# Products of weight and one-hot for every other chunk moved from VectorE to GpSimd, in the first of two gate builds

## What is computed

```python
def peer_ffn(xn, w_query, sub_keys, expert_u, expert_v):   # 16384 experts
    ...   # 8 heads; top 16 of 128 x 128 keys: expert_idx and gates, 128 per token
    u = expert_u[ib]                                  # rows gathered by token
    act = jax.nn.gelu(jnp.einsum('ced,cd->ce', u, xb))
    return jnp.einsum('ce,ced->cd', gb * act, expert_v[ib])
```

## Time and profile of the kernel before

| | us |
|---|---|
| three runs | 2079.51, 2079.55, 2066.76 |
| their median | 2079.51 |
| the profiled execution | 2073.71 |
| span in its profile | 2072.0 |

### The profile page before, as it was taken

The page is one execution under the profiler, slowest core; times in us unless marked ns, Lnnn a source line. Parts: engine busy times, 40 slices in busy tenths (PEclk is TensorE's granted clock), DMA queues, the critical chain, the costliest instruction groups (busy, mean ns, idle before and its releaser), DMA issues.

```text
span 2072.0 us, 23875 instructions
## 1 busy us (share of the span) xinstructions
PE 1931.7 (93%) x8967; PEld 1250.0 (60%) x8967; DVE 1206.6 (58%) x3046; ACT 414.7 (20%) x963; POOL 876.8 (42%) x785
## 2 busy tenths in 40 slices
PE   8999999999989999998898498999999889999998
PEld 7688886855865888884767376444435543333333
DVE  0123101002997888887886999978768784444321
ACT  2233210121202454121211122100003330101102
POOL 0000000000775433543445555654657777556643
PEclk9999999999989999999999558999999999999999
DMA  7343444433999887999897768999999999999997
GB/s 250 105 134 110 143 162 134 130 122 122 344 391 355 299 265 240 376 386 328 326 315 287 279 214 264 337 409 409 409 409 353 369 355 400 409 409 409 409 389 284
DMA packets 252439, 613.47 MB, mean 296 GB/s; under 512 B 18676, under 2 KB 121124, under 8 KB 252324
## 3 DMA queue, kind: packets, MB, share of 16 engines
q0 software_dynamic: 110592, 402.70, 51.7%
q1 hardware_dynamic: 141120, 208.17, 28.7%
q10 hardware_dynamic: 612, 1.07, 0.2%
HBM read 609.77 MB, written 2.10 MB: 295 GB/s over the span
## 4 chain that ended last, share of the span: by engine, by line
PE 63%; DMA 16%; DVE 12%; POOL 4%; issue 2%; ACT 2%; SPq 0%; POOLq 0%; DVEq 0%; ACTq 0%
PE ps L595 27%; PE ps L853 10%; PE ps L816 8%; PE ps L608 7%; DMA u_rows<-in_peer_u_dram,idx 6%; DVE u_rows L1328 5%; DMA v_rows<-in_peer_v_dram,idx_turned 3%; POOL u_rows L554 2%; DMA wring<-in_w_in_dram 2%; PE ps L631 2%; DMA wring<-in_peer_w_query_dram 2%; PE ps L843 2%; POOL v_rows L568 2%; DVE hot_a L1382 2%; PE ps L620 1%
## 5 line engine op out<-in xcount | busy, mean ns | idle before, releaser
L554 POOL DMA_INDIRECT u_rows<-in_peer_u_dram,idx x512 | 596.4, 1165 | 1008.8 <-DVE idx L1315 520.6
L1328 DVE CUSTOM_DVE_ANT_0 u_rows<-u_rows,xn 128x1024 f32<-128x1024 f32 x512 | 622.0, 1215 | 173.1 <-DMA u_rows<-in_peer_u_dram,idx 169.7
L595 PE MATMUL ps<-xT,wring 128*128 128x256 f32 x2432 | 556.9, 388 | 23.4 <-DMA wring<-in_w_in_dram 11.0
L595 PEld LDWEIGHTS ps<-xT,wring 128*128 128x128 f32 x2432 | 465.6, 194 | 93.8 <-DMA wring<-in_w_in_dram 12.8
L853 PE MATMUL ps<-d_rows,gates 128*128 128x512 f32 x1024 | 456.0, 599 | 0.0
L853 PEld LDWEIGHTS ps<-d_rows,gates 128*128 128x128 f32 x1024 | 190.0, 190 | 266.0 <-issue 266.0
L816 PE MATMUL ps<-v_rows,diag 64*64 64x512 f32 x1928 | 248.8, 633 | 19.9 <-DMA v_rows<-in_peer_v_dram,idx_turned 15.5
L843 PEld LDWEIGHTS ps<-hot_b,hot_a 128*128 128x128 f32 x1024 | 148.4, 232 | 61.2 <-DVE hot_b L1390 31.3
L568 POOL DMA_INDIRECT v_rows<-in_peer_v_dram,idx x121 | 133.0, 1099 | 122.5 <-PE ps L816 100.8
L843 PE MATMUL ps<-hot_b,hot_a 128*128 128x64 f32 x1024 | 156.7, 320 | 24.6 <-DVE hot_b L1390 24.5
L816 PEld LDWEIGHTS ps<-v_rows,diag 64*64 64x64 f32 x1928 | 68.9, 138 | 157.2 <-issue 132.7
(11 more groups left out here) (197 smaller groups left out, 1711.5 us busy)
## 6 DMA issues: line engine op xcount, KB each, us to landing
wring<-in_w_in_dram SPq DMA_DIRECT2D x128, 512.0 KB, 5.6
d_rows<-in_peer_v_dram SPq DMA_DIRECT2D x128, 512.0 KB, 6.8
wring<-in_peer_w_query_dram SPq DMA_DIRECT2D x32, 512.0 KB, 8.2
wring<-in_w_branch_conv_dram SPq DMA_DIRECT2D x16, 512.0 KB, 6.4
wring<-in_w_branch_attn_dram SPq DMA_DIRECT2D x16, 512.0 KB, 5.9
wring<-in_w_out_dram SPq DMA_DIRECT2D x16, 512.0 KB, 6.4
wring<-in_xattn_wq_dram SPq DMA_DIRECT2D x16, 512.0 KB, 8.1
wring<-in_xattn_wo_dram SPq DMA_DIRECT2D x16, 512.0 KB, 6.5
```

What stands on the lines that cost most here:

```text
L554: pool.indirect_dma_start(out=u_rows[:, n % URING, :], out_offset=None, in_=peer_u[0], in_offset=bass.IndirectOffsetOnAxis(ap=experts_of(g ...
L595: mm = pe.matmul(bank(job)[:, 0:HN], w[:, k % 4, P * b:P * (b + 1)], act[:, k, :], start=(k == 0), stop=(k == KT - 1))
L1328: dve.tensor_tensor_reduce(out=u, in0=u, in1=(xn2 if h else xn1)[:, i, :], scale=1.0, scalar=0.0, op0=ALU.mult, op1=ALU.add, accum_out=dot ...
```

## The change

GpSimd makes the product of `hot_b` and the weights for the odd chunks 1, 3, ... 31 of the first build. It does so in its loop at n = CH_SLOT[ch] + 8, behind the u gather and the v gathers of that step; the gather of that step waits for the dot of slot CH_SLOT[ch], the slot in which VectorE makes the one-hots of ch. The product waits for `hot_half`. A new semaphore `hot_pool` counts GpSimd's products, and TensorE waits for one or the other. VectorE's one_hots ends for these chunks with the second one-hot. The second build is unchanged.

```diff
     CH_SLOT = spread(12, 46, 32) + spread(151, 177, 32)
+    BY_POOL = range(1, 32, 2)
...
+        def wait_hots(eng, ch):
+            if ch in BY_POOL:
+                eng.wait_ge(hot_pool, BY_POOL.index(ch) + 1)
+            else:
+                eng.wait_ge(hot_rdy, sum(c not in BY_POOL for c in range(ch + 1)))
+
+        def weigh(eng, ch):
+            i, o = 8 * (ch % 32) // P, 8 * (ch % 32) % P
+            eng.wait_ge(hot_half, ch + 1)
+            return eng.tensor_tensor(hot_b[:, ch % 2, :, :], hot_b[:, ch % 2, :, :],
+                                     wT[:, i, o:o + 8].unsqueeze(2).to_broadcast([P, 8, 64]), ALU.mult)
...
                     ).then_inc((v_ready if kind == "v" else u_ready)[place], 16)
+                for ch in BY_POOL:
+                    if CH_SLOT[ch] + URING == n:
+                        weigh(pool, ch).then_inc(hot_pool, 1)
...
             def gate_chunk(ch):
-                pe.wait_ge(hot_rdy, ch + 1)
+                wait_hots(pe, ch)
...
-                dve.wait_ge(hot_half, ch + 1)
-                dve.tensor_tensor(hot_b[:, ch % 2, :, :], hot_b[:, ch % 2, :, :],
-                                  wT[:, i, o:o + 8].unsqueeze(2).to_broadcast([P, 8, 64]),
-                                  ALU.mult).then_inc(hot_rdy, 1)
+                if ch not in BY_POOL:
+                    weigh(dve, ch).then_inc(hot_rdy, 1)
```

More of the change, by code:

```diff
@@ L379, in build_trunk @@
         hot_rdy = sem("hot_rdy")
+        hot_pool = sem("hot_pool")
         wb_done = sem("wb_done")
```

## The result

The changed kernel takes 2079.41 us (median of 22 runs); the kernel before, run beside it, 2072.77 (22 runs). The ratio is 1.0032 with a 95% interval of 1.0020 to 1.0044, that is +6.6 us (4 to 9): a small loss, clear of the noise. The median of the three runs that I started from (2079.51) lay high in the spread of before (2065 to 2088).

The account below looks back on a forecast made before the run. VectorE was taken to bound the first gate build, transfers what follows. Saving 11.5 us and losing 14.6 gave +3.1, so 2076.8 us from the profiled 2073.71, moved towards the three-run median to 2078; range 2061 to 2091.

Parts of the forecast that it names:

- VectorE sets the pace, transfers behind follow one to one: First build: VectorE busy 132.16 of 135 us; time saved or lost there moves everything behind by as much.
- Saved: 16 x 0.72 = 11.5 us: First build: 16 of 32 products leave VectorE, 0.72 us each, the most the change can bring.
- Exclusion is real, and most of its price is VectorE's: GpSimd's products and VectorE's two-input instructions make each other stand; VectorE loses 16 x 1.25 - 5.4 = 14.6 us.
- the walk: VectorE's 16 slots behind odd chunks, checked for one-input work that can run beside GpSimd's product: 5.4 us of cover.
- TensorE costed at nothing: First build: moved chunks ready about 1.7 us later, 0.9 us of slack at half clock, so no wait.
- Sum: Loss of 14.6 us less 11.5 saved gives +3.1, so 2076.8 us from the profiled 2073.71.
- the likeliest case: Exclusion with a small net cost, its own range 2071 to 2087 us; chance 0.50.
- rival B: Late products make TensorE the bound at half clock: +11, 2085 us, VectorE's waits 8 us or more; chance 0.12.
- B's upper form: TensorE's gaps also keep the clock low, 10 pairs' periods of 11.0 us for 8.8: another 22, 2107 us; chance 0.03.
- Rival A: GpSimd and VectorE don't exclude each other; VectorE keeps 11.5 us less 1 to 3, giving 2064 us; chance 0.27.
- C: GpSimd's product is slow, 3.2 us; VectorE loses 34 us, giving 2108 us; chance 0.05.
- D: Gain in the build lost behind it, full DMA engines setting the end; within 2 us of before; chance 0.06.

Follow-up runs that it names:

- none: The changed kernel with the odd chunks' products left out on every engine, so the output lacks those weights; 2059.16 us against 2072.95 before, ratio 0.9943.
- first: The changed kernel with GpSimd's product moved ahead of the v gathers of its step; 1.0019 of the kernel before.
- split_b: The kernel before with ScalarE multiplying four of eight tokens of every first-build chunk, VectorE the other four, run a second time; 0.9984 of before.

## Why the prediction was right or wrong

- **VectorE sets the pace, transfers behind follow one to one.** Right: the stage's differences arrive, from -11.5 to +12.3 us.
- **Saved: 16 x 0.72 = 11.5 us.** Right, measured 11.52 with the products left out.
- **Exclusion is real, and most of its price is VectorE's.** Right in mechanism. In the changed kernel it costs 132.20 - 121.86 = 10.3 us of VectorE's time; the sum had 14.6. The product's own length was taken as 1.25 us and is 1.05. With 1.05 the sum of the prediction would have been 16 x 1.05 - 5.4 = 11.4, near the 10.3, in part by luck. One thing was not foreseen: TENSOR_SCALAR and CAST with one input stand too (590 and 584 ns in the mean of two for 170), and the walk had counted them as cover; MAX8, FIND_INDEX8 and MATCH_REPLACE8 don't. On the other side, two of the late products (1251.28 and 1279.43) ran while VectorE waited for TensorE and cost it next to nothing.
- **TensorE costed at nothing.** Here the prediction failed. VectorE is not busy for 9.95 us in place of the 2.42 of none, so 7.5 us more, and its waits for TensorE alone grow from 0.2 to 8.1 us. The step treated a moved chunk as regularly 1.7 us late; it is 1.3 at the least, and that is nearly absorbed (first: 1.5 us of waits). It left out the place of the product in GpSimd's queue: behind gathers, v gathers among them which themselves wait for pairs (7.7 us), six of sixteen products came 2.3 to 3.2 us later than VectorE's had. With the product ahead of the v gathers VectorE's idle time is 5.76 us, so some 4.2 of the 7.5 go with the order and 3.3 stay. The prediction even said that the order "gather, v gathers, product" changes, and asked only whether gathers come late, not whether the product does. It also took the clock for risen from 1240 on by one window of the earlier trace rows; two later windows of the same trace, shown above, have 0.61 and 0.50. What the half clock adds to a late chunk is not separated from the order by any run.
- **Sum.** -11.5 + 10.3 + 7.5 = +6.3 us. This adds up by construction, since both prices are differences to none; that it is the right stage shows in the time, +6.6 beside +6.35. Predicted was +3.1, from two errors of opposite sign (exclusion 4.3 too high, lateness 7.5 missing). The price falls between the likeliest case and rival B (+11), with part of B's mechanism at work, and the prediction's own sign for B, waits of 8 us or more, is met (8.1). But B had the lateness before the clock's first rise, and all five waits came after it, the first at 1226.6. Of B's upper form, chunk, pair and chunk in 11.0 us at the half clock, one such period is the 10.9 us above.
- **The number.** The sum was made against 2073.71 and then moved towards a median of three runs, 2079.51. 22 runs put before at 2072.77. So 2078 read as -1.5 us against the median shown, though my own sum said slower: the step from the sum to the number gave its sign away. That 2078 lies 1.4 us from the measured 2079.41 is luck: a shift of 1.2 us taken from the noise of three runs made up part of the 3.2 us missing in the sum. The time lies in the stated range, and the change is within 1%.
- **Rival A** (no exclusion) is out: VectorE's busy time would be 122 us. C is out (1.05, not 3.2 us). D is out for the moves on GpSimd; for ScalarE's split (split_b) about half of the gain is lost behind the stage.

## What to carry to other kernels

Work handed from a saturated VectorE to GpSimd is, here, paid back nearly in full (10.3 of 11.5 us), because GpSimd reads SBUF while VectorE runs two-input instructions: count the helper's length against what is saved, less only the VectorE work that is seen to run beside it, and prefer an engine or a form (writes alone, ScalarE) that does not meet it. Look where the handed-over work stands in the helper's queue, how long the instructions ahead of it last and what they wait for. And base a forecast of half a percent on the profiled execution's own sum; the median of three lay as far off (6.7 us) as the effect is large (6.6).

## What the runs showed of the hardware

- A product of 128x512 in float32 on GpSimd takes 1.05 us when it begins first, a copy 0.61; two-input VectorE instructions stand during either, and the product stands during theirs; whichever stands has the standing time inside its recorded duration (dot 2.06 for 1.22, or 1.63 beside a copy, product 1.96 for 1.05). The Trainium skill ("SBUF — State Buffer", section Who interferes with whom) states this rule, and these runs agree, with memsets, which only write (1.2 us, dots still 1.22), as the exception that it names.
- Beside the product a TENSOR_SCALAR and a CAST of 16 columns lasted 1.0 us in place of 0.17, while MAX8 (two in 0.48), FIND_INDEX8 (0.28, in first) and MATCH_REPLACE8 (0.27) kept their length.
- 8 TENSOR_SCALAR instructions of 64 columns with two scalars by partition cost 0.22 us each in sequence, 1.79 us in all, more than 512 columns in two instructions (1.32 us).
